# Prompt compression placed between the projection's products, attention's programs in the projection's block, constants loaded after the first tile

## The reference, cut to what matters

```python
xn = rms_norm(x, norm1_g)
z = xn @ w_in                       # q, kv (6 slots), gates, and the recurrence's columns
q = rms_norm(q.reshape(B, L, 8, 64), q_norm_g)
# compress_block, on blocks of 32 raw rows of kv slots 0 and 1:
h = gelu(einsum('bnjgd,jde->bnge', rows, w1))
out = einsum('bnge,ef->bngf', h, w2)
ck, cv = rms_norm(out_k, k_norm_g[0]), out_v          # 32 blocks of the prompt
# per head: softmax over ck, over selected keys, over a window of 512 keys
o = gate0 * o_cmp + gate1 * o_sel + gate2 * o_win
```

## Time and profile before

| | us |
|---|---|
| median of three runs | 2065.01 |
| the profiled execution, its own time | 2064.16 |
| its span in the profile | 2062.5 |
| PE busy | 1938.3 (94%) |
| DVE busy | 870.4 (42%) |
| ACT busy | 585.1 (28%) |
| POOL busy | 149.7 (7%) |
| mean granted TensorE clock | 0.962 of full |

### The profile page before, as it was taken

The page is one execution under the profiler, slowest core; times in us unless marked ns, Lnnn a source line. Parts: engine busy times, 40 slices in busy tenths (PEclk is TensorE's granted clock), DMA queues, the critical chain, the costliest instruction groups (busy, mean ns, idle before and its releaser), DMA issues.

```text
span 2062.5 us, 38066 instructions
## 1 busy us (share of the span) xinstructions
PE 1938.3 (94%) x15625; PEld 1760.9 (85%) x15625; DVE 870.4 (42%) x1702; ACT 585.1 (28%) x1203; POOL 149.7 (7%) x213
## 2 busy tenths in 40 slices
PE   6899969999986899879999999999999999999999
PEld 4668656676673789769999999999999999999998
DVE  6233025666603177633223334644244424442443
ACT  5133135665512124332212222221112111111121
POOL 4000001100030043310000000000000000000000
PEclk8899958999998899989999999999999999999999
DMA  8422553000066310233221122111111111111112
GB/s 238 70 71 64 223 123 119 7 2 2 2 202 231 105 34 24 55 75 83 77 77 49 36 83 82 52 41 41 51 51 43 41 54 46 51 39 53 41 51 85
DMA packets 164891, 148.18 MB, mean 72 GB/s; under 512 B 7769, under 2 KB 152138, under 8 KB 163698
## 3 DMA queue, kind: packets, MB, share of 16 engines
q1 hardware_dynamic: 156852, 126.39, 20.5%
q0 software_dynamic: 6208, 17.67, 3.4%
q10 hardware_dynamic: 1696, 2.22, 0.4%
HBM read 120.54 MB, written 29.99 MB: 73 GB/s over the span
## 4 chain that ended last, share of the span: by engine, by line
PE 54%; DMA 0%; DVE 0%; ACT 0%; issue 0%; SPq 0%; DVEq 0%
PE psum L246 18%; PE psum L247 18%; PE psum L248 18%; DMA state_rows<-in_state_conv 0%; PE psum L850 0%; DMA out_y_prompt<-ys 0%; PE psum L745 0%; PE psum L840 0%; PE psum L800 0%; DVE ys L725 0%; DVE hl L688 0%; DVE hid L684 0%; DVE t_wl L580 0%; ACT hh L518 0%; DVE conv_state L576 0%
## 5 line engine op out<-in xcount | busy, mean ns | idle before, releaser
L247 PE MATMUL psum<-xgl,t_wh 128*128 128x344 f32 x1056 | 338.2, 320 | 0.0
L246 PE MATMUL psum<-xgh,t_wh 128*128 128x344 f32 x1056 | 338.0, 320 | 0.0
L248 PE MATMUL psum<-xgh,t_wl 128*128 128x344 f32 x1056 | 337.3, 319 | 0.0
L247 PEld LDWEIGHTS psum<-xgl,t_wh 128*128 128x128 f32 x1056 | 198.6, 188 | 0.1
L248 PEld LDWEIGHTS psum<-xgh,t_wl 128*128 128x128 f32 x1056 | 198.4, 188 | 0.0
L246 PEld LDWEIGHTS psum<-xgh,t_wh 128*128 128x128 f32 x1056 | 198.2, 188 | 0.1
L246 PE MATMUL psum<-hh,t_wh 128*128 128x344 f32 (+2 forms) x456 | 146.3, 321 | 2.0 <-DVEq L686 1.7
L248 PE MATMUL psum<-hh,t_wl 128*128 128x344 f32 (+2 forms) x456 | 145.9, 320 | 0.0
L247 PE MATMUL psum<-hl,t_wh 128*128 128x344 f32 (+2 forms) x456 | 145.8, 320 | 0.0
L246 PE MATMUL psum<-wh_n,xh 128*128 128x512 f32 (+3 forms) x288 | 112.7, 391 | 18.6 <-DVE wl_n L962 18.6
L580 DVE TENSOR_TENSOR t_wl<-t_raw,t_wh 128x1024 fp32r<-128x1024 f32 (+1 forms) x93 | 112.9, 1214 | 33.7 <-ACT t_wh L499 28.6
(11 more groups left out here) (445 smaller groups left out, 3921.6 us busy)
## 6 DMA issues: line engine op xcount, KB each, us to landing
t_raw<-in_w_gate SPq DMA_DIRECT2D x22, 512.0 KB, 3.8
t_raw<-in_w_up SPq DMA_DIRECT2D x22, 512.0 KB, 3.8
t_raw<-in_w_down SPq DMA_DIRECT2D x24, 384.0 KB, 3.3
cmp_pages<-in_cache_kv SPq DMA_DIRECT2D x64, 128.0 KB, 2.2
t_raw<-in_w_in SPq DMA_DIRECT2D x16, 512.0 KB, 4.0
raw_n<-in_w_in SPq DMA_DIRECT2D x24, 256.0 KB, 3.8
r_raw<-in_w_in SPq DMA_DIRECT2D x12, 512.0 KB, 3.9
xh_copy<-xh SPq DMA_DIRECT2D x1, 4128.0 KB, 13.5
```

Of the source, the lines that this page charges most:

```text
L246: pe.matmul(out, wh, xh, start=(first and k == 0), stop=False)
L247: pe.matmul(out, wh, xl, start=False, stop=False)
L248: mm = pe.matmul(out, wl, xh, start=False, stop=(last and k == n - 1))
```

## The change

- `project_tokens` and `project_nsa` take the compression (`comp`), `bias_tiles` and attention's five programs as arguments. `attend_prompt` no longer opens blocks: it returns its programs (`tensor`, `vector`, `scalar`, `sync`, `gpsimd`), and each engine calls its own at the end of its projection program. Two barriers go.
- The compression moves into steps of weight tile j = 2. PE does half of the small matmuls after step 19, half after step 20, the next products after step 21, the sum of squares after step 22. ACT's three parts follow its work of steps 20, 21 and 22, and DVE's two parts follow steps 22 and 23. It uses PSUM banks 5 and 6 in place of 4 and 5.
- POOL's DMAs of the compression's weights and of the constants wait for the first normed tile (`ready` 1).
- The memset of half of `bias_tiles` goes from DVE to POOL, ahead of step 9's store. SP loads the other half before it copies `xh` and `xl` out.
- `keep_sample_rows` moves into DVE's unit 8 of attention.
- Buffers are laid out anew: `bias_tiles` and `pt` lie where the tables' constants were.

```diff
@@ project_nsa: act_tile, dve_tile, pe_tile, pool_tile
+        project_act(act, n, j, tt, z)
+        if n == FIRST_C + 1:
+            comp.act_first(act, 0)
+        elif n == FIRST_C + 2:
+            comp.act_second(act, 0)
+        elif n == FIRST_C + 3:
+            comp.act_third(act, 0)
...
+        project_dve(dve, n, j, tt, z, z_free)
+        if n == FIRST_C + 3:
+            comp.dve_first(dve, 0)
+        elif n == FIRST_C + 4:
+            dve.wait_ge(tables.S["all"], 7 * 16)
+            comp.dve_last(dve, 0)
...
+        if n == FIRST_C:
+            pe.wait_ge(ev, 2 * NTT)
+            pe.wait_ge(tables.S["wts"], 8 * 16)
+            pe.wait_ge(tables.S["all"], 7 * 16)
+        if n in (FIRST_C, FIRST_C + 1):
+            comp.pe_first(pe, 0, n - FIRST_C, 2)
+        elif n == FIRST_C + 2:
+            comp.pe_second(pe, 0)
+        elif n == FIRST_C + 3:
+            comp.pe_third(pe, 0)
...
+        if n == NTT:
+            pool.memset(bt[:, :, 0:256], 0.0).then_inc(bt_in, 16)
         if n == 3:
+            pool.wait_ge(ready, 1)
             tables.weights(pool)
             tables.pool_later(pool)
@@ project_nsa: the ends
-        act.activation(c.gates[:, 0:8, :], c.gates[:, 0:8, :], ACT.Sigmoid)
-        act.activation(c.gates[0:NS, 8, :], c.gates[0:NS, 8, :], ACT.Sigmoid)
+        act.activation(c.gates[:, 0:8, :], c.gates[:, 0:8, :], ACT.Sigmoid).then_inc(gate_on, 1)
+        act.activation(c.gates[0:NS, 8, :], c.gates[0:NS, 8, :], ACT.Sigmoid).then_inc(gate_on, 1)
+        at_act(act)
+    def pe_end(pe, z_free):
+        pe.wait_ge(ev, NSTEP)
...
+        pe.wait_ge(z_free, NALL)
+        at_pe(pe)
+    def dve_end(dve):
+        dve.wait_ge(gate_on, 2)
+        at_dve(dve)
+    def sp_end(sp, z_done):
+        sp.wait_ge(tables.S["w"], 16)
+        sp.dma_start(bt[:, :, 256:512], toeplitz).then_inc(bt_in, 16)
         sp.dma_start(c.xh_dram, ...)
         sp.dma_start(c.xl_dram, ...)
+        sp.wait_ge(kept, 16)
+        sp.wait_ge(z_done, NALL)
+        at_sp(sp)
@@ attend_prompt: vector, sync
+        dve.wait_ge(bt_in, 32)
...
+                if i == 0 and u == 8:
+                    keep_sample_rows(c, dve)
...
         sp.wait_ge(c.kept, 32)
+        sp.wait_ge(comp.S["p1"], 1)
```

More of the change, by code:

```diff
@@ L1022, in project_nsa @@
     kept = c.sem("n_kept")
+    gate_on = c.sem("n_gate_on")
+    at_pe, at_dve, at_act, at_sp, at_pool = attention
     c.kept = c.sem("x_kept")
@@ L2017, in attend_prompt @@
     s_c = c.low("s_cmp", [P, 2, 2, 32])
[L2018 removed]
+    pt = nc.alloc_sbuf_tensor_at("pt", [P, 2, 8 * P], F32, offset=pt_at)
     rsb = c.low("rsb", [P, 2, 3 * P])
@@ new lines, in scalar, with expo, evac, evac_spread @@
+    def scalar(act):
+        def expo(u, kind):
+            qt, r, k0, nw, ncmp = shape(u)
+            q = u % 2
+            b, s, w = {"cmp": (0, s_c, ncmp), "sel": (1, ss, (qt + 1) * P), "win": (2, sw, nw * P)}[kind]
+            done = reds[chunk_no(u, kind)]
+            for g in range(GROUPS):
+                act.wait_ge(S["red"], done - 1 + g)
+                act.activation(s[:, q, g, 0:w], s[:, q, g, 0:w], ACT.Exp, bias=lows[:, q, g, b:b + 1], scale=-1.0,
+                               accum_out=den[:, q, g, b:b + 1]).then_inc(S["ex"], 1)
+        def evac(u, i):
+            G = first_group[u] + i
+            act.wait_ge(S["tp"], turned[G] + 1)
+            if G >= 2:
+                act.wait_ge(S["pv"], G - 1)
+            for x, n, m in pieces(u, i, 0):
+                act.activation(pt[0:m, G % 2, x * P:(x + n) * P], c.psum[0:m, TB, x * P:(x + n) * P], ACT.Copy).then_inc(S["ev_a"], 1)
+        def evac_spread(u):
+            n = place[u, "spread"]
+            act.wait_ge(S["sp"], u + 1)
+            if u >= 2:
+                act.wait_ge(S["om"], u - 1)
+            act.activation(rsb[:, u % 2, :], c.psum[:, SB + 2 * (n % 2), 0:3 * P], ACT.Copy).then_inc(S["ev_r"], 1)
+        for kind in chunks(0):
+            if kind != "far":
+                expo(0, kind)
+        for u in range(NU):
+            n, at, later = steps(u)
+            for i in range(n):
+                evac(u, i)
+                for kind in later.get(i, []):
+                    expo(u + 1, kind)
+            evac_spread(u)
+            for kind in later.get(n, []):
+                expo(u + 1, kind)
@@ new lines, in sync @@
+    def sync(sp):
+        sp.wait_ge(c.kept, 32)
+        sp.wait_ge(comp.S["p1"], 1)
+        for n in range(4):
+            sp.dma_start(c.w1k[32 * n:32 * n + 32, :, :], io["phi_k_w1"][0]).then_inc(early, 16)
+            sp.dma_start(c.w1v_a[32 * n:32 * n + 32, :, :], io["phi_v_w1"][0, :, 0:HD // 2, :]).then_inc(early, 16)
+        for x in range(NS * 8):
+            page = sp.value_load(c.pages[0:1, x:x + 1], min_val=0, max_val=io["cache_kv"].shape[1] - 1)
+            sp.dma_start(c.cmp_pages[:, x, :], pg_flat[bass.ds(page, 1), :, 0:256].rearrange("o t c -> (o t) c")).then_inc(early, 16)
+        sp.wait_ge(early, 16 * (8 + NS * 8))
@@ L2346, in attend_prompt, with gpsimd @@
+    def gpsimd(pool):
+        for u in range(NU):
+            qt, r = divmod(u, R)
+            o = c.o_nsa[:, r, qt * P:(qt + 1) * P]
+            t = tmp[:, u % 2, :]
+            pool.wait_ge(S["om"], u + 1)
+            pool.tensor_tensor(t[:, 0:P], t[:, 0:P], t[:, P:2 * P], ALU.add).then_inc(S["oa"], 1)
+            pool.wait_ge(S["oa"], 2 * u + 1)
+            pool.tensor_tensor(o, t[:, 0:P], t[:, 2 * P:3 * P], ALU.add).then_inc(S["oa"], 1)
     c.base = low0
+    return tensor, vector, scalar, sync, gpsimd
```

450 lines of the change are left out of this document (189 added, 261 removed).

## The result

| | us | lowest to highest | runs |
|---|---|---|---|
| before | 2065.54 | 2064.51 to 2066.19 | 4 |
| changed | 2041.85 | 2040.69 to 2042.61 | 4 |
| ratio | 0.9885 | 95%: 0.9868 to 0.9902 | |

The change takes 23.7 us off the median. The forecast was 28.1, to 2037.0, and the result lies inside its range of 2025.5 to 2047.0. The two profiled executions, 2064.16 and 2042.61 of own time (spans 2062.5 and 2041.0), are 21.55 apart.

A forecast was written before the change was run, and what follows sets the result against it. PE was taken to bound the kernel (54% of the last-ending chain), with time available where it idles or runs at lower clock. Savings 23.6 - 8.7 - 0.3 + 12.0 - 0.5 + 2.0 = 28.1 us; median 2037.0, range 2025.5 to 2047.

The forecast's parts named there:

- Part 1: Gap between last product and attention's first Exp: first Exp near 263.75 in place of 287.39, saving 23.6 us.
- Part 2: Compression inserted between products of j = 2: costs 8.7 us, between 7.9 and 15.8; square root's table load 0.3 more.
- Rival B: Compression's small pairs keep 54 ns each, costing 6.4 us more: 2043.4; chance 8%, the skill's form included.
- Part 3: Projection's first step without the constants' DMA traffic: saves 12.0 us, bounds 5 and 13.5.
- Part 4: The rest: nine copies in unit 8 cost 0.5 us, memset nothing, attention's first units gain 2.0.
- clock's term: Attention's first units, starting at full clock: gain of 2.0 us, bounds 10 down to -2.
- Rival A: PE's clock holds through attention's start, adding 8 us to the gain: 2029; chance 20%.
- a change behind attention: Sign of a wrong prediction: stages behind attention changing in length; no size given.
- C: First step's loads not freed, the ring's slices slow for another reason; saving 4, not 12: 2045; chance 10%.
- D: Joined block gains nothing at the gap; attention waits for `bias_tiles` or pages' `kept`, some 12 us later: 2049; chance 6%.
- E: Lower clock lasts in attention, 4.6 us more per unit; with eight units 2073.8; chance 4%.

The follow-up runs named there:

- e4: Changed kernel with the compression put back behind the last product, blocks still joined: 2047.01 us, ratio 0.9901 to the kernel before.
- e8: Changed kernel with the compression behind the last product and an added early POOL drain: 2037.78 us, ratio 0.9856 to the kernel before.
- e3: Kernel before, with only POOL's wait for the first normed tile ahead of the constants added: 2057.34 us, ratio 0.9948.
- e11: Changed kernel with early POOL drain, compression behind the last product and medium filling of PE with idle matmuls: 2040.53 us, ratio 0.9862 to the kernel before.
- e5: The changed kernel run again, unaltered: 2042.83 us, ratio 0.9880 to the kernel before.
- e6: Changed kernel with one POOL drain added before attention, timed a second time: 2039.91 us, ratio 0.9867 to the kernel before.
- e1: Changed kernel with one POOL drain added between its last projection DMA and attention: 2039.83 us, ratio 0.9865 to the kernel before.
- e12: Changed kernel with early POOL drain, and SP issuing nine of POOL's copies in the first block: 2037.92 us, ratio 0.9856 to the kernel before.
- e2: Changed kernel without POOL's wait for the first normed tile, so constants issue at once: 2056.38 us, ratio 0.9941 to the kernel before.
- e7: Changed kernel with early POOL drain and heavy filling, 144 idle matmuls on PE at attention's start: 2053.44 us, ratio 0.9929 to the kernel before.

## Why the prediction was right, point by point

- **Part 1, the gap, 23.6:** 23.65 measured. The reading of the chain (sigmoids, table load, Exp) was right to a tenth. Its account of the barriers was not: the prediction took them as gone with their waits. The 3.57 us that POOL's drain held the first one were work that the kernel still owed, and it paid 3.53 of them at attention's end. This is the step that failed. It is a term that the sum hasn't got, worth more than any other error in it. The rows were in the trace of before: a drain of 3568 ns at 263.0 and one of 562 at 572.8.
- **Part 2, 8.7 and 0.3:** 8.98. The pairs took 7.86 for my 7.5. The two steps with pairs grew by 4.04 and 4.05, the two behind them by 0.66 and 0.23, in which the square root's table load lies. Rival B is out: 30.7 ns a pair. The Trainium skill ("TensorE: Matmul & The Clock Gate", section "Wait — 56ns, not 53.3ns?") has its 62 ns a matmul for hardware decode off, and the trace shows no such bound here. But what the move buys was misread. The cost that I put against it, 9.0, was compared with a gap that held the pairs cold. e4 and e8 show that they are warm behind the last product too once the barrier is gone, so the price of 13.87 in the gap came from the wait at the barrier.
- **Part 3, 12.0:** 12.15 from the first slice on, 11.22 counted with the 0.93 by which the block began later. That start moves from run to run (38.67 to 40.60 in fourteen traces), mostly with the end of POOL's drain in the block before, and is no effect of the change. e3 shows the term alone: 10.4 us in the median and 10.6 at the same place of the trace (123.07 us from the first low part to the end of j = 1's products, against 133.63 before). All twelve kernels with the late constants take 121.3 to 123.3 us for it, so the term is 10.3 to 12.3 us, and that the profiled execution shows the 12.0 of the forecast so closely is in part luck. Further on the spread grows: by the last product e3, e4, e8 and e11, whose projections are alike, take 210.11, 209.12, 207.36 and 212.41 us from the first low part, or 8 to 13 less than before. Some show PE at 0.83 in 60 to 70 (e4, e11), some at 1.00 (e8).
- **Part 4:** the copies cost 0.34 for 0.5, the memset nothing. The clock's term, +2.0, gave +0.87 in this trace, and its sign is not sure: the six copies from unit 0's to unit 5's span 37.24 us before, 36.45 in the change, and 37.06, 38.85, 38.31 and 39.29 in e5, e6, e1 and e12. It isn't the early drain that makes the longer ones, since e2 and e3, which have none, take 38.9 too. Rival A fell (0.50 from 265 on), by the mechanism that the prediction gave for the fall: PE waits as the engines start up. e7 shows that the other outcome could be had.
- **Not foreseen:** 1.08 us less for the slices of j = 3, 0.7 of it in PE's waits for them, and about 2.5 lost behind the samples' start. The change and e5, the same program, take 1490.3 and 1487.7 us from the samples' first matmul to the end, and before 1487.9, so I take the latter for the spread of single executions, though the prediction had named a change behind attention as a sign of being wrong. The 1.08 has no run of its own.
- **Rivals C, D and E** did not happen: C by e2 and e3, D by the first Exp 3.8 us after the last product's end, E by unit 5 at 5.5 us.

The forecast of 2037.0 was 4.9 below the median. The drain is 3.5 of it, the clock's term 1.1.

## What to carry to other kernels

A barrier that is removed takes away its waits but not what an engine does at it: look in the queues' rows for each engine's own drain. If one is long, see first whether DMAs were still under way when it began. If none were, ask where it will be paid next, and let the engine do it while the others work. Before moving work off a cold gap, ask what made the gap cold; if the barrier did, removing it may be enough, and the work can stay. DMAs that nobody needs soon belong behind the loads that the first step waits for: one wait was worth 10 of the 24 us.

## What the runs showed of the hardware

- When all of POOL's 43 DMAs had landed, its queue took 3.57 us to drain right behind the landing (before, e1, e3, e6 to e12) and 4.08 when it drained only 288 us after the last issue (the change). It took 0.56 at attention's end when it had issued none since its last drain.
- With DMAs under way POOL's drain ended behind the last landing: 0.5 us behind it in the first block, 0.2 in e12, where it took 8.0, and 1.35 in the samples' block, where it took 3.8 to 5.5.
- SP's drains took 0.01 to 0.38 us, also with its copies still under way.
- Pairs of weight load and 32-column matmul (a 64x64 float32 weight tile) run at 30 to 31 ns each at a clock of 1.00 and 54 ns at 0.50.
- A float32 matmul of 128x128 by 128 columns costs PE 0.24 us at a clock of 1.00 (e7). It is a dear way to keep the clock up: 44 of them bought 5 to 8 us of attention's start and some 2 us of the kernel, which isn't clear of the spread.
- In the change PE waited 0.92 and 1.85 us at attention's start, and the granted clock was 1.00, 0.61 and 0.50 in three windows of 5 us from 255 on. It stayed at its lower level to about 290, with PE busy 2.9 to 4.5 of each 5 us. Before, it was at 0.50 even from 320 to 325, where PE was busy throughout. In e11, where PE was filled, it was at 0.50 in 265 to 270 and at 1.00 from 270 on.
